# A 1 MB weight load moved earlier in the transfer queue of a gated convolution and pooling block

## The reference

```
h = rmsnorm(x, norm_mix)
proj = h @ w_in + b_in        # conv_val, conv_gate, pool_in, gate_a, gate_b: 1024 columns each
u  = causal_dwconv(conv_val * sigmoid(conv_gate), 31 taps)
ya = silu(layernorm(u)) @ conv_w_out
yb = pool_branch(pool_in) * pool_scale
merged = sigmoid(gate_a) * ya + sigmoid(gate_b) * yb
x = x + merged @ mix_w_out
x = x + gdfn(rmsnorm(x, norm_ffn))     # up, conv over 3, gelu(a) * b, down (D_FF = 2816)
out = rmsnorm(x, norm_final)
```

## Time and profile before

| | us |
|---|---|
| median of 3 runs | 1274.51 |
| lowest and highest | 1273.81 and 1274.82 |
| the profiled execution | 1273.25 |
| its span, first to last instruction | 1271.5 |
| TensorE busy in it | 1258.7 |

### The profile page before, as it was taken

The page is one execution under the profiler, slowest core; times in us unless marked ns, Lnnn a source line. Parts: engine busy times, 40 slices in busy tenths (PEclk is TensorE's granted clock), DMA queues, the critical chain, the costliest instruction groups (busy, mean ns, idle before and its releaser), DMA issues.

```text
span 1271.5 us, 15705 instructions
## 1 busy us (share of the span) xinstructions
PE 1258.7 (99%) x5718; PEld 1044.9 (82%) x5718; DVE 1040.3 (82%) x1228; ACT 524.7 (41%) x754; POOL 893.9 (70%) x618
## 2 busy tenths in 40 slices
PE   9999999999999999999999999999999999999997
PEld 8888888888888887778888888888888888888887
DVE  5899999999999787998698766767766779887975
ACT  6222222324334693443354434344334345424551
POOL 3566748676787726757739887787787776667862
PEclk9999999999999999999999999999999999999999
DMA  9443231334234467741304223233223269868923
GB/s 360 146 137 124 90 133 54 131 122 171 99 100 134 148 235 248 262 166 71 129 34 144 104 91 110 92 122 116 92 91 114 86 217 349 327 238 302 368 77 133
DMA packets 85741, 199.23 MB, mean 157 GB/s; under 512 B 6176, under 2 KB 27680, under 8 KB 81568
## 3 DMA queue, kind: packets, MB, share of 16 engines
q1 hardware_dynamic: 81216, 187.73, 41.7%
q10 hardware_dynamic: 4448, 10.49, 2.2%
HBM read 147.08 MB, written 51.12 MB: 156 GB/s over the span
## 4 chain that ended last, share of the span: by engine, by line
PE 87%; DVE 4%; DMA 3%; POOL 2%; ACT 2%; issue 1%; SPq 0%; DVEq 0%; POOLq 0%; ACTq 0%
PE ps L3033 29%; PE ps L3035 29%; PE ps L3034 29%; DMA cv<-in_x 1%; DMA raw<-in_wstream 1%; POOL w_lo L1324 1%; DVE res L2634 1%; DMA h_lo<-g_kept 1%; DMA w_lo<-sums_kept_t 1%; PE ps L3097 0%; DVE h_lo L2609 0%; ACT w_hi L1698 0%; DVE cv L2499 0%; DVE ga L2634 0%; DVE hi_f L2417 0%
## 5 line engine op out<-in xcount | busy, mean ns | idle before, releaser
L3033 PE MATMUL ps<-h_lo,w_hi 128*128 128x512 f32 (+1 forms) x852 | 329.2, 386 | 1.7 <-DMA w_lo<-prep_kept_t 1.1
L3035 PE MATMUL ps<-h_hi,w_hi 128*128 128x512 f32 (+1 forms) x852 | 327.3, 384 | 0.0
L3034 PE MATMUL ps<-h_hi,w_lo 128*128 128x512 f32 (+1 forms) x852 | 327.3, 384 | 0.0
L3033 PEld LDWEIGHTS ps<-h_lo,w_hi 128*128 128x128 f32 x852 | 160.0, 188 | 36.2 <-issue 3.4
L3035 PEld LDWEIGHTS ps<-h_hi,w_hi 128*128 128x128 f32 x852 | 160.0, 188 | 31.9
L3034 PEld LDWEIGHTS ps<-h_hi,w_lo 128*128 128x128 f32 x852 | 160.1, 188 | 31.5
L2328 DVE SCALAR_TENSOR_TENSOR ps<-tmp,par,ps 128x512 f32<-128x512 f32 x224 | 158.2, 748 | 0.0
L3033 PE MATMUL ps<-ga_r,w_hi 128*128 128x512 f32 (+1 forms) x335 | 129.9, 388 | 0.3 <-issue 0.3
L3035 PE MATMUL ps<-cv_r,w_hi 128*128 128x512 f32 (+1 forms) x335 | 129.5, 387 | 0.0
L3034 PE MATMUL ps<-cv_r,w_lo 128*128 128x512 f32 (+1 forms) x335 | 129.5, 387 | 0.0
L1214 POOL TENSOR_TENSOR w_lo<-raw,w_hi 128x1024 fp32r<-128x1024 f32 x25 | 62.7, 2509 | 89.3 <-ACT w_hi L1615 89.2
(11 more groups left out here) (332 smaller groups left out, 2827.3 us busy)
## 6 DMA issues: line engine op xcount, KB each, us to landing
raw<-in_wstream SPq DMA_DIRECT2D x44, 512.0 KB, 3.6
tmp<-in_wffn SPq DMA_DIRECT2D x14, 1024.0 KB, 4.9
g_kept<-res SPq DMA_DIRECT2D x21, 512.0 KB, 2.9
res<-in_wffn SPq DMA_DIRECT2D x10, 1024.0 KB, 4.7
ga_r<-g_kept SPq DMA_DIRECT2D x18, 512.0 KB, 6.8
h_lo<-g_kept SPq DMA_DIRECT2D x17, 512.0 KB, 6.3
res<-in_xT SPq DMA_DIRECT2D x7, 1024.0 KB, 5.9
cv<-in_wffn SPq DMA_DIRECT2D x12, 512.0 KB, 5.4
```

The lines of the kernel that those rows point to most:

```text
L3033: nc.tensor.matmul(out, a_hi, b_lo, start=start, stop=False, skip_group_check=onto)
L3034: nc.tensor.matmul(out, a_lo, b_hi, start=False, stop=False, skip_group_check=onto)
L3035: return nc.tensor.matmul(out, a_hi, b_hi, start=False, stop=stop, skip_group_check=onto)
```

## The change

The load of mix block 1 stood behind the two stores of the last gate tile. It now stands behind the load for (P1,2), ahead of the loads for (P1,3) and (P2,0) and of the two stores. Its own wait (`f_wlo` at 42), its source, its place in `raw` and every other instruction are as before.

```diff
@@ -1028,9 +1028,10 @@
             keep_pooled(KT - 2)
             load_conv((P1, 1))
             load_pooled(KT - 1)
-            load_conv((P1, 2), (P1, 3), (P2, 0))
+            load_conv((P1, 2))
+            load_mix_block(1, f_wlo, GATE_OPS)
+            load_conv((P1, 3), (P2, 0))
             keep_gate(KT - 1)
-            load_mix_block(1, f_wlo, GATE_OPS)
             load_conv((P2, 1), (P2, 2))
```

## The result

The changed kernel is slower. The median went from 1273.83 us (21 runs) to 1276.15 us (21 runs, 1273.46 to 1278.37), a ratio of 1.0017 with a 95% interval of 1.0011 to 1.0023, or +2.2 us. The forecast was a gain of 0.5 us in a range up to 1275.7. So the two traces differ by more than the kernels do, and I compare places in them, not their ends.

A forecast was written before the change was run, and what follows sets the result against it. TensorE was taken as the bound, with late starts at (P2,1) and (P6,0) costing 1.8 us; 1.2 of that went back to a new wait, leaving 1274.51 - 0.55 = 1274.0 us, range 1272.4 to 1275.7.

The forecast's parts named there:

- What bounds the kernel: TensorE, nearly without gaps behind this stage, so time changed before 490 us passes to the end; late starts cost 1.8 us.
- Price of the block, 3.0 us: The 1 MB mix block occupies the DMA engines for about 3.0 us, at the high end 4.4 us.
- SyncE: Block issued at about 462.2 us with its own wait already met; cost nothing, cover 0.9 us.
- (P1,3): Its weights land at 471.9 against a need at 471.53, so TensorE stalls about 0.4 us (0 to 1.8).
- The stores: Two gate-tile stores land 1.8 us later, at 473.9; with 0.4 us slack, conv_t2_high(0) starts 1.4 us later.
- the idle share: Idle DMA time in 466 to 470 us, credited with absorbing 1.2 us of the block's 3.0 us ahead of the stores.
- (P2,3): TensorE waits about 1.0 us there for ScalarE's conv_first(3), itself 1.4 us later.
- With the same 2.87 us TensorE starts (P6,0) at 486.2 or 486.3: ScalarE takes (P6,0) at 483.4; TensorE follows 2.87 us later instead of at 486.81, leaving a gain of 0.5 to 0.6 us.
- Gain if nothing else turns late: 1.8 us: Both waits, at (P2,1) and (P6,0), go because the block is no longer ahead of their loads; 1.8 us.
- slower through the stores: Rival: stores land behind a crowded queue, conv_t2_high(0) starts late; +0.8 to +0.9 us at the bound, 1275.4; chance 0.20.
- point of balance: In the stores rival: from 2.0 us of delay, stores landing after 474.5, the change costs more than was won.
- The page of the Trainium skill that I had cited against the change: HBM access takes 2 us at high load; stores up to 1.8 us later again, turning -0.55 into about +1.2 us.

The follow-up runs named there:

- e5_half: Changed kernel with only the first half of block 1 (512 KB) early, the second half behind the load for (P4,0); 1275.62 against 1274.29 us for the kernel before, ratio 1.0010.
- e6_after_dve: Changed kernel with the low part of (P6,0) made by VectorE behind conv_t_low("T1") instead of by GpSimd; 1273.93 against 1274.29 us for the kernel before, ratio 1.0003.
- e1_late: Kernel before with mix block 1 loaded still later, behind the loads for (P5,0) and (P5,1); 1274.0 against 1274.01 us, ratio 0.9998.
- e10_late2: Kernel before with only block 1 moved, behind the load for (P4,0); 1273.45 against 1273.44 us, ratio 1.0000.
- e4_act_delay: Kernel before, transfers untouched, with ScalarE making the copy of conv_first(1) four times instead of once; 1276.24 against 1274.01 us, ratio 1.0019.
- e3_act_stores: Changed kernel with the two stores of the last gate tile issued by ScalarE, on another queue; 1276.4 against 1274.01 us for the kernel before, ratio 1.0021.
- e9_before_dve: Kernel before, block 1 at its old place, with only the low part of (P6,0) moved from GpSimd to VectorE; 1273.4 against 1273.44 us, ratio 0.9996.

## Why the prediction was wrong

- **What bounds the kernel.** Right in the large: time lost here passes to the end. (One slip of words: (P2,1) is the product right behind (P2,0), the second behind (P1,3); the sum 476.97 starts from (P1,3) and is right.) Wrong for (P6,0): I took its releaser, GpSimd, for a step of fixed length behind ScalarE and did not ask why a step of 1.30 us had taken 2.01.
- **Price of the block, 3.0 us.** Right: the low half for (P1,3) took 2.9 us longer, the later store 3.0 us.
- **SyncE.** Right in its cost: the block was issued at 462.6 (462.2 forecast), later because the issue ahead of it took 1.37 us instead of 0.43, and the issues behind it kept their distance to TensorE.
- **(P1,3).** Right: a wait of 0.47 us (about 0.4 forecast).
- **The stores.** `conv_t2_high(0)` started at 474.13 (473.9 forecast), and that agreement is luck. The later store took 3.0 us longer, not 1.8: none of the 1.2 us that I had let the idle share absorb was absorbed. The slack of 0.4 us was about right, since the stores and ScalarE's steps both follow its last sigmoid. So the stores cost 2.5 us of ScalarE's time and not 1.4. How much is absorbed is not fixed: nothing here, 0.1 of the 1.5 us in e5_half, and the full 1.2 us in e6_after_dve (1.8 us longer), where the block was issued earlier and the stores later.
- **(P2,3).** Right: a wait of 0.93 us for `conv_first(3)` (1.0 forecast).
- **"With the same 2.87 us TensorE starts (P6,0) at 486.2 or 486.3."** This step failed. The start was 488.39, 4.84 us behind ScalarE and not 2.87, since GpSimd's part ends only about 1.1 us after VectorE's run, which the stores had shifted with everything else. e1_late, e10_late2, e4_act_delay and e6_after_dve show it.
- **"Gain if nothing else turns late: 1.8 us."** Failed for the same reason: e1_late and e10_late2 take both causes away and gain nothing. With a credit of 0 instead of 1.8 us, the sum of my own terms would have been +1.3 us. The idle share that absorbed nothing makes up the rest, 1.2 us, less about 0.5 by which ScalarE was earlier in this trace than before, counted from TensorE's last gate product: about +2, as (P6,0) shows.
- **The rivals.** The right one was "slower through the stores", with the same chain as the forecast, and it had 0.20. Its point of balance was set at 2.0 us of delay; by the runs it is near none, and each us costs one, as the fixed 14.27 us show.
- **The rest.** Counted from the last gate product, (P6,1) starts 2.1 us later than before in the two traces; by 568 us it is 4.3 us. Between lie three more waits for GpSimd's low parts, 1.9 us in all. Two of them (0.3 to 0.6 us) are in e3_act_stores and e4_act_delay as well, and two of 0.8 (for VectorE) and 0.4 us are in e1_late, which lost nothing by its median; so they are not what tells the kernels apart. The third, 0.93 us at 540.34, stands in the changed kernel's profile alone, and what sets it stays open.

The page of the Trainium skill that I had cited against the change, on the latency of HBM under load, was not needed: the stores took 3.0 us longer, what the bytes ahead of them account for, and 1.4 us with half of the bytes. The page that mattered, of the Trainium skill too, I had passed over. The traces show GpSimd's step ending 1.1 to 1.2 us after VectorE's run in all kernels where it makes this part, whatever its own start. The Trainium skill, "SBUF — State Buffer", section "Who interferes with whom", says that a VectorE instruction with two SBUF inputs and a GpSimd instruction that reads SBUF contend, as VectorE's second input comes through the read interface that the two share; that the shared pair is an exclusive lock; and, of VectorE's 2-port modes, that whoever issues first has it for the whole instruction while the other blocks fully. The traces agree as to the blocking; that it is this port, no run here shows. They go further in one point: the part begun at 482.43 in e1_late came to its end only behind three VectorE instructions in a row, not behind the one that was running.

## What to carry to other kernels

When a wait is taken away, ask what the waiting instruction would have met next, and look for a step there that ran longer than its like does alone: its end may be another engine's end. A transfer moved forward is paid by everything that it is put ahead of, stores too, and where a store's landing frees a buffer, the engine that waits for the buffer pays. Compare places in two traces by their distance from a common instruction ahead of the change: here the traces were up to 0.8 us out of step, as much as the effects. And do not credit the idle share of the DMA engines ahead of such a transfer as absorbed: of 1.2 us that I had credited, one trace absorbed nothing and another all of it.

## What the runs showed of the hardware

- A GpSimd subtraction of 128 by 512 with both inputs in SBUF took 1.30 us alone and 3.67, 3.99 and 4.02 us beside a run of VectorE's subtractions from SBUF (e1_late, changed kernel, e4_act_delay). It ended 1.1 us or a little more after the run in each. With a shorter overlap it ends as far behind the run: it took 2.01 us when it began 0.85 us ahead of the run's end (kernel before). In e9_before_dve its next part began behind the run and took 1.30 us. VectorE makes the same part in 0.68 us.
- Stores issued from ScalarE's queue shared the backlog of SyncE's queue: 6.3 us to landing at a DMA share of 0.88 to 1.06, where they took 2.1 and 2.6 us at a share of 0.50 in the kernel before. Here a second issuing engine did not get its transfers past those of the first.
